# Experts sorted by token count: five narrower lanes in two slots a trip, and their first loads in the routing stage

## The reference

```python
scores = sigmoid(h @ router_w)                       # 512 x 64
choice = scores + router_bias
# the 4 best of 8 groups of experts, by the sum of their two best choices,
# and of what they hold the 8 best experts: sel
w = scores[sel] / scores[sel].sum(-1) * 2.5
y = sum over the 8 chosen e of  w_e * ((silu(h @ gate_e) * (h @ up_e)) @ down_e)
y = y + (silu(h @ sh_gate) * (h @ sh_up)) @ sh_down  # shared expert
out = rms_norm(x + g2 * y)
```

## Time and profile before

| | |
|---|---|
| median of 3 runs | 2342.8 us (2341.57 to 2345.9) |
| profiled execution, its span | 2343.3 us |
| PE, DVE, ACT, POOL busy | 92%, 57%, 20%, 17% of the span |
| routing stage | from about 1606 to 1665.5 us |
| experts, first gate-up product to last down product | 1681.7 to 2265.2 us |
| combining, to the end | about 2269 to 2343 us |
| trips of three slots | 17 |

### The profile page before, as it was taken

How to read it: one execution, slowest core, us unless ns; L and a number is a source line. 1 busy time by engine, 2 the same in 40 slices (tenths; PEclk the granted TensorE clock), 3 DMA queues, 4 the chain that set the end, 5 groups by cost and what they waited for, 6 DMA issues and landing times. The chain is left out here.

```text
span 2343.3 us, 27600 instructions
## 1 busy us (share of the span) xinstructions
PE 2151.4 (92%) x10395; PEld 1246.3 (53%) x10395; DVE 1330.6 (57%) x2524; ACT 461.2 (20%) x916; POOL 396.7 (17%) x771
## 2 busy tenths in 40 slices
PE   6999989999999999999879999998699999999975
PEld 3444554777785458883443788445333333333322
DVE  3448863766672134434968333535766766767745
ACT  2013561121120011004235232011011111111111
POOL 0005000111000000000000000000444444444433
PEclk9999999999999999999989999998799999999988
DMA  9422000535524015981111100401499999898976
GB/s 389 180 81 81 36 1 20 233 144 216 215 81 179 36 72 229 391 306 54 37 57 58 51 3 4 177 36 54 180 372 397 425 353 421 344 407 357 413 281 252
DMA packets 68999, 446.60 MB, mean 191 GB/s; under 512 B 12276, under 2 KB 12932, under 8 KB 44066
## 3 DMA queue, kind: packets, MB, share of 16 engines
q0 software_dynamic: 36176, 254.42, 27.1%
q1 hardware_dynamic: 32722, 190.78, 21.0%
HBM read 416.27 MB, written 73.45 MB: 209 GB/s over the span
## 5 line engine op out<-in xcount | busy, mean ns | idle before, releaser
L965 PE MATMUL psum<-arena 128*128 128x256 f32 x1904 | 416.7, 381 | 2.1 <-PEq L1005 2.0
L2824 PE MATMUL psum<-arena 128*64 128x512 f32 (+1 forms) x1088 | 366.1, 600 | 38.9 <-DVE arena L2872 16.6
L965 PEld LDWEIGHTS psum<-arena 128*128 128x128 f32 x1904 | 361.4, 190 | 62.6 <-issue 14.0
L2872 DVE STREAM_TRANSPOSE arena<-arena 32x256 f32<-32x256 f32 x832 | 362.1, 435 | 15.8 <-DMA arena<-scratch_h,arena 4.1
L2824 PEld LDWEIGHTS psum<-arena 128*64 128x64 f32 (+1 forms) x1088 | 143.8, 165 | 226.6 <-issue 197.7
L2815 PE MATMUL psum<-arena 128*64 128x512 f32 (+1 forms) x544 | 186.2, 598 | 1.2 <-ACT arena L2850 1.2
L1067 PE MATMUL psum<-arena 128*128 128x512 f32 x352 | 151.8, 592 | 0.3 <-PEq L1091 0.3
L2815 PEld LDWEIGHTS psum<-arena 128*64 128x64 f32 (+1 forms) x544 | 68.5, 163 | 113.2 <-issue 111.8
L869 PE MATMUL psum<-arena 128*128 128x512 f32 x256 | 111.2, 593 | 2.3 <-DVE arena L2432 1.5
L1067 PEld LDWEIGHTS psum<-arena 128*128 128x128 f32 x352 | 66.6, 190 | 83.4 <-issue 83.4
L2878 DVE COPY arena<-psum 128x512 f32<-128x512 f32 x51 | 35.3, 692 | 132.7 <-PE psum L2815 132.7
(11 more groups left out here) (521 smaller groups left out, 2932.0 us busy)
## 6 DMA issues: line engine op xcount, KB each, us to landing
scratch_expert_out<-arena SPq DMA_DIRECT2D x18, 2048.0 KB, 19.9
scratch_expert_out<-arena SPq DMA_DIRECT2D x51, 512.0 KB, 9.9
arena<-in_w_ada SPq DMA_DIRECT2D x12, 2048.0 KB, 16.8
arena<-in_ada_w POOLq DMA_DIRECT2D x12, 2048.0 KB, 8.8
arena<-in_w_up SPq DMA_DIRECT2D x22, 1024.0 KB, 4.8
arena<-in_w_in SPq DMA_DIRECT2D x9, 2048.0 KB, 11.0
arena<-in_w_down SPq DMA_DIRECT2D x5, 2048.0 KB, 8.6
arena<-in_w_o SPq DMA_DIRECT2D x2, 2048.0 KB, 8.4
```

What stands on the lines that cost most here:

```text
L965: last = pe.matmul(out, w[:, k, :], x[:, k, :], start=(k == 0), stop=(k == KH - 1))
L2824: last = pe.matmul(K.bank[2 + s][r, :], xt[:, s, P * k + r.start:P * k + r.stop], gu[:, lane, 2 * E_FF * k:2 * E_FF * (k + 1)], start=(k = ...
L2872: last = dve.transpose(channels[c:c + 32, :, a:a + 32], tokens[a:a + 32, :, c:c + 32])
```

## The change

Routing sorts the experts by their token counts. Small ones go to narrow lanes of 32 rows, large ones to wide lanes of 64 rows: an expert takes as many successive pieces of its lane kind as it needs. N is the smallest number of trips at which those that sort below 64 N narrow rows and the rest fit 192 N wide rows. The sums over sorted experts are made by PE, with comparisons of keys (64 x count + number) instead of scans on VectorE, and N by 128 trials at once, one on each partition.

A trip has two slots of 128 rows: slot 0 has a lane of 64 rows and two of 32 (its products run as four tiles of 32 rows, the first two of which share weights), slot 1 has two lanes of 64. So each trip has five lanes, each with its own buffers, and ten weight loads are issued in it. Buffers of the tokens and of their transposes are two instead of three. POOL's order is now: gather of slot n, gate-up weights of n-1, down weights of n-2, each for the next use; VectorE's: transposes of slot n, product of n-1, move out of n-2.

In routing, POOL clears the token buffers and loads the first gate, up and down weights of slot 0 as soon as the table of sources is there, then gathers both slots' first tokens when the lists are. VectorE makes the weights of the experts at the end of that stage. The one-hot operands are made eight blocks at a time, with the scaling on ACT. PE sums the lists in four parts with gate-up products of the shared expert between them, and runs the shared expert's down products after the lists instead of before. In the second projection's stage 8 fills of 2 MB are stored instead of 18.

```diff
-            parts = [LANE * lane + t for lane in range(UNROLL) for t in range(8, LANE, NT)]
+            parts = [TRIPS * slot + t for slot in range(UNROLL) for t in range(T * TOP // (UNROLL * P), TRIPS, NT)]
...
-                fill(3)
+                fill(2 if n < 6 else 0)
...
-BLOCK = P
-BLOCKS = 96
-UNROLL = 3
+UNROLL = 2
+TRIPS = 32
+BLOCKS = UNROLL * TRIPS
 BIG = 1.0e30
-LANES, LANE = 4, 32
 NOWHERE = 1.0e6
-RC_LOWER, RC_TOKEN, RC_LANE, RC_TRIP, RC_ROW, RC_TWOS, RC_EXPERT, RC_COUNT, RC_N = 0, 64, 68, 69, 70, 71, 103, 167, 295
+NARROW = 8192.0
+LANES = [(0, 0, 64), (0, 64, 32), (0, 96, 32), (1, 0, 64), (1, 64, 64)]
+NL = len(LANES)
+OF_SLOT = [[n for n, lane in enumerate(LANES) if lane[0] == s] for s in range(UNROLL)]
...
+    K.gu, K.down = [sb(f"e_gu{n}", [P, KD * 2 * E_FF]) for n in OF_SLOT[0]], [sb(f"e_down{n}", [P, 2 * D]) for n in OF_SLOT[0]]
...
+            gate_up(1, 4, 5)
+            pe.wait_ge(trial.sem, 1)
+            trial_mm.by(pe.matmul(K.bank[0][:, 0:2], K.ones[:, :], num[:, 2:4], start=True, stop=True))
+            gate_up(1, 5, KD)
+            pe.wait_ge(starts_in.sem, 1)
+            starts_mm.by(pe.matmul(K.bank[2][:, 0:NL * TRIPS], K.ones[0:EXPERTS, :], starts[0:EXPERTS, :, :].rearrange("p l t -> p (l t)"), start=True, stop=True))
             gate_up(2)
-            gate_up(3)
-            pe.wait_ge(eb_done.sem, 1)
-            eb_t.by(pe.matmul(K.bank[3][:, 0:P], K.ones[:, :], diag[:, :], start=True, stop=True))
+            pe.wait_ge(sg_act.sem, 1)
+            for t in range(NT):
+                pe.wait_ge(hot.sem, t + 1)
+                for j in range(TOP):
+                    last = pe.matmul(K.bank[4][:, 0:BLOCKS], within[:, t % 2, j, :], place[:, t % 2, j, :], start=(t + j == 0), stop=(t == NT - 1 and j == TOP - 1))
+                list_mm.by(last)
+                gate_up(3, 2 * t, 2 * t + 2)
...
+                act.wait_ge(equal.sem, t + 1)
+                hot.by(act.activation(place[:, t % 2, :, :], place[:, t % 2, :, :], ACT.Copy, scale=const[:, RC_TOKEN + t:RC_TOKEN + t + 1]))
...
+            link(pool, pool.memset(K.xg[:, :, :], 0.0), K.cleared)
+            pool.wait_ge(K.sourced.sem, 1)
+            load_weights(K, pool, 0, 0, 0)
+            load_weights(K, pool, 1, 0, 0)
+            pool.wait_ge(K.listed.sem, 1)
+            for s in range(UNROLL):
+                gather_rows(K, pool, 0, s)
...
+            for t in range(NT):
+                if t >= 2:
+                    dve.wait_ge(list_mm.sem, t - 1)
+                row_in, block_of = (part[:, n, TOP * t:TOP * t + TOP].unsqueeze(2) for n in range(2))
+                step(tt(place[:, t % 2, :, :], count[:, 0:BLOCKS].unsqueeze(1).to_broadcast([P, TOP, BLOCKS]), block_of.to_broadcast([P, TOP, BLOCKS]), ALU.is_equal))
+                link(dve, tt(within[:, t % 2, :, :], count.unsqueeze(1).to_broadcast([P, TOP, P]), row_in.to_broadcast([P, TOP, P]), ALU.is_equal), equal)
...
+def load_weights(K, pool, down, i, s, back=0):
+
+    to, ready, landed = (K.down, K.down_ready, K.down_in) if down else (K.gu, K.gu_ready, K.gu_in)
+    src = K.dram["exp_down" if down else "exp_gu"].rearrange("e p n -> (e p) n")
+    lanes = OF_SLOT[s]
+    index = K.wrows[:, down, lanes[0]:lanes[0] + len(lanes)]
+    pool.tensor_copy(index.unsqueeze(2), K.source[:, lanes[0]:lanes[0] + len(lanes), trip_of(-back, i)]).then_inc(ready.sem, 1)
+    blocks_done(pool, ready, i, s, -UNROLL * back)
+    pool.tensor_tensor(K.wait_for[:, 4:5], K.rstd[:, 0:1], K.rstd[:, 0:1], ALU.add)
+    for lane in lanes:
+        offset = bass.IndirectOffsetOnAxis(ap=K.wrows[:, down, lane:lane + 1], axis=0)
+        pool.indirect_dma_start(to[lane][:, :], None, src, offset, bounds_check=EXPERTS * P - 1, oob_is_err=False).then_inc(landed[lane].sem, 16)
+
+
...
+    tiles = [[(slice(a, a + 32), n) for n in OF_SLOT[0] for a in range(LANES[n][1], LANES[n][1] + LANES[n][2], 32)],
+             [(slice(LANES[n][1], LANES[n][1] + 64), n) for n in OF_SLOT[1]]]
...
+            def refill(down, i, s, off, used=None):
                 b = (s + off) % U
+                back = -((s + off) // U)
+                if used is None:
+                    blocks_done(pool, down_mm if down else gu_mm, i, s, off - U)
+                else:
+                    pool.wait_ge(down_mm.sem, used)
+                pool.tensor_tensor(K.wait_for[:, 5:6], K.rstd[:, 0:1], K.rstd[:, 0:1], ALU.add)
+                load_weights(K, pool, down, i, b, back)
+
+            load_weights(K, pool, 0, 0, 1)
+            load_weights(K, pool, 1, 0, 1)
 
             def step(i, s):
+                first = isinstance(i, int)
+                blocks_done(pool, turned, i, s, -U)
+                pool.tensor_tensor(K.wait_for[:, 6:7], K.rstd[:, 0:1], K.rstd[:, 0:1], ALU.add)
+                gather_rows(K, pool, i, s)
+                if not (first and U * i + s < 3):
+                    refill(0, i, s, -1)
+                if not (first and U * i + s < 4):
+                    refill(1, i, s, -2)
+
+            def rest(n):
+                refill(0, n, U - 1, 0)
+                refill(1, n, U - 1, -1, pool.value_load(K.table[0:1, 1:2], min_val=1, max_val=U * TRIPS - 1))
+                refill(1, n, U - 1, 0)
+
+            steps(pool, step, rest, 1)
```

501 lines of the change are left out of this document (233 added, 268 removed).

## The result

The changed kernel takes 2353.64 us (median of 18 runs, 2347.69 to 2359.59), beside 2345.31 us (18 runs, 2333.78 to 2349.19) of the kernel before on the same chip. The ratio is 1.0037, 95% interval 1.0027 to 1.0046: slower by 0.4%, or 6 to 11 us. The forecast was 2353.6 and slower. The profiled execution has a span of 2353.6, 10.3 above that of before.

A forecast was written before the change was run, and what follows sets the result against it. PE sets the pace, DMA a close second. Slots -68.1, weight waits +63.4, clock +20, routing +1.1, its second slot -2, 3.6 given back: +10.8 on the median 2342.8, forecast 2353.6 us, range 2318 to 2377.

The forecast's parts named there:

- Slots: Expert stage: 44 slots at 10.9 us in place of 51 at 10.74, -68.1 us.
- Rival (d): Expert stage: four tiles with different moving data run two abreast, doubling slot 0's products; 2465 us, chance 0.02.
- Weights: Expert stage: gate-up weights come late for two or three new lanes; 89 us of waits for 25.6, +63.4.
- Landing in a full queue: Expert stage weight loads: the last part of a load's time, taken as 4.5 us, bounded by 2.4 and 5.0.
- rival (b): Expert stage: landing takes 2.4 us or less and most two-lane waits vanish; 2314 us, chance 0.18.
- It is the unevenness.: Expert stage: waits come from a full queue in even trips and an idle one in odd, not from total bytes.
- The clock: Expert stage: eleven waits reach 4.5 us, each gate-up behind them 2.8 us slower; 31, two thirds counted, +20 us.
- Rival (a): Expert stage: the waits for weights come but the clock does not fall; 2333.6 us, chance 0.17.
- Routing: Routing stage: shorter chain to the lists, shared down products behind them; first expert gate-up +1.1 us, ends -4 and +5.
- Loads moved ahead "shorten nothing": Routing stage: early first weight loads gain nothing, as the first gate-up waits for VectorE's transposes, not weights.
- Skipped loads: Expert stage: 11,000 more small packets from skipped weight loads cost 0 us, as DMA idles then; 9 as upper end.
- Rival (c): Expert stage: dearer waits, landing at 5.5 us, skipped loads in the path, full clock cost; 2378 us, chance 0.15.

The follow-up runs named there:

- the last variant of the new layout: Three of four groups of VectorE's expert weights computed before the lists, against the changed kernel with order, shift and down-product edits: 2315.47 us, ratio 0.9873.

## Why the prediction was right, point by point

**Slots.** -68.1, and -2 for the second slot: measured -70.9 in the stage without loads on either side. The count of 44 and 51 was right. The pace was 10.95, not 10.90: three changes of shape at 0.11 each over the 10.62 of a slot without, not 0.09. Rival (d) is out: four tiles with different moving data take 7.07. (Its price was also added wrongly: 2353.6 + 231 - 110 is 2475, not 2465.)

**Weights.** The sum had five waits of 10.0, seven of 5.0, and 4 for down weights: 89, of which 3.6 were given back. Measured are five of 8.7 to 11.3 (50.5), six two-lane ones of slot 0 (26.0), and 4.3 and 0.4 in slot 1: 81.2. But for the 0.4 they are in the trips that the layout on paper named. The 25.6 taken off for the kernel before was right in size; 3.2 of it is one wait for VectorE's product and not for weights. The two-lane waits were a little smaller than 5.0 on the mean (4.3), and down weights never came late: that term is 0. Landing in a full queue was the crux. With rival (b)'s 2.4 or less most two-lane waits vanish; they didn't, so it falls. The fixed 2.0 us a DMA that the Trainium skill gives (DMA: Bandwidth & Descriptors, Anatomy of one DMA) would have made about 58 us of waits by the forecast's estimate, and the trace has 81.2, so it doesn't price a load in this queue. The runs measure the sum of start, transfer and landing: for three lanes 24.5 to 29.3 us from release to products in the changed kernel and 25.0 to 26.0 without the down loads, for a forecast of 24.7. The start in it was 3.9 at most slots and not 4.5; from the first issue to the products it was 21.1 to 22.1 without the down loads, where the forecast has 20.2. That 4.5 of it is landing is argued from the earlier trace rows and the idle engines at the earlier trace rows, not shown by itself.

**"It is the unevenness."** Right in part. Taking 49 of 191 MB away takes 11.5 us of waits, shifting one lane kind by a piece brings 15 us and the order 14.5. What the phrase leaves out is the lead: with no slot of three new lanes left, the 17 slots with two still wait, 1.6 to 4.7 us and three times 6.7 to 7.8, as 14.8 us of lead don't hold them.

**The clock.** Slow gate-ups cost 22.0, forecast 20. Rival (a) falls: eleven waits of 3.9 us and more were each followed by a gate-up of 8.4 to 9.8, and those of 1.28 and 0.42 by one of 7.1. The size was right for another reason than the one given. The forecast had each slow gate-up cost 2.8 and a third of it won back by the queue. The slow gate-ups themselves cost only 1.3 to 2.8, 2.0 on the mean, and waits and slow gate-ups added up without anything won back. That the two thirds hit it is luck.

**Routing.** The step that was mis-sized, within its stated ends of -4 and +5. Forecast +1.1, measured +4.7 in this profile, and +2.7 to +3.3 in five variants that share it. Taking 5.4 off for the later start: the lists' products began at 1644.0, where the working has them from about 1642, but ended near 1660.6 in place of 1655. The last two groups took 1.9 where 1.8 was written, the first two 3.65 and 2.65, and a round with its quarter of gate-up took 7.0, 4.3 and then 3.5. The rows above say why: the clock was at 0.50 from 1649 to 1657, behind a wait of 5.27. The forecast priced the clock in the expert stage and put it at nothing here. The down products then took 14.0 and not 15.7: in before they ran at a granted clock of 0.89 (1642 to 1658) and here at full. What the working said at the end, that it would be some 9 less if these products were not last, was 4.5 to 6.5 when tried.

**Loads moved ahead "shorten nothing".** Wrong as a statement on this kernel (26 us), without effect on the sum: the comparison was with the old layout, where the first slot waited for VectorE, and in the changed kernel it does so again. I priced the edit against the old stage and not against the new layout without it.

**Skipped loads.** 0 us, with 9 as upper end. Packets under 512 B were 24,227 in this profile and 12,276 in that of before: 12,000 more, where the forecast has 11,000. Outside the waits they cost nothing: in the kernel in which all later loads are skipped, the slots keep their 10.95. Within the waits a part may be theirs, and no run took them away alone. Rival (c) falls with the size of the waits.

**The total.** -70.9 - 25.4 + 81.2 + 22.0 is +6.9 for the stage (+6.6 read directly), +2.7 to +4.7 for routing: +9 to +12, forecast +10.8. The medians differ by 8.3. The stages of before are from one execution, and the +2.5 of the later start would come on top, so some 1 to 6 us of the terms are not accounted for. The forecast stood on a median of 2342.8 for before, and this one's is 2345.3, so a part of the agreement to 0.1 us is chance; the agreement of the terms is not.

## What to carry to other kernels

Fewer and fuller steps shorten the compute but also the time between a buffer's release and its next use; work out that lead against the largest single refill, step by step, not the mean bandwidth. Where refills come in bursts, look first at which groups change together and at what is issued ahead of them on the same queue: an offset of one piece and another order of issue were worth 30 us here, more than three times what the re-layout lost. A loader that waits for one consumer holds up everything it issues for the others, so moving an issue is priced by every wait that it now stands behind. And products behind a wait of some 5 us were slow in the routing stage as in the expert stage: price the clock wherever an edit makes the matrix engine stand still.

## What the runs showed of the hardware

**The clock after short waits.** In the earlier trace rows waits of up to 2.5 us left the clock at 1.00. That is not a rule. In the shifted kernel (rows above) a wait of 3.70 was followed by a gate-up of 7.07, and one of 2.01 by 8.79. In the old layout with the gather between the loads:

```profile
1777.46 8.78 PE L2824 MATMUL psum<-arena 128*64 128x512 f32 x32 [2.05 <-issue]
...
1881.23 7.09 PE L2824 MATMUL psum<-arena 128*64 128x512 f32 x32 [2.62 <-issue]
```

Over the slots of these profiles after the first three, 154 waits for weights were longer than 0.5 us. Behind the 40 below 1.7 us the gate-up always took 7.1, behind the 51 above 3.70 always 8.3 to 10.0, and of the 63 between them 25 were followed by one of 7.1 and 38 by a slow one (four of these had a wait of 3.5 to 3.9 for VectorE's product just before). So a wait of 1.9 to 3.7 us has two prices in these runs, 0 and mostly 1.7 us more, and its length alone doesn't tell which. The forecast treated 2.5 as free and 4.66 as dear, and all of its eleven waits lay above the band.

**A stage's end behind gathers.** In the last variant of the new layout VectorE had nothing left to do for 7.56 us and POOL still went on only 4.09 us after it had issued its second gather. At the same place of the kernel before, where no gather stands ahead, POOL began the next stage at 1666.02, 0.5 us after VectorE's last instruction. In this program that looks like time that no work taken off another engine buys back; a run that moves the gathers would show it.
